# FFN1's pair stage: highs and lows of the tokens in one 512-column matmul, and both halves of a bank added by ScalarE's copy and VectorE

## What is computed

```
x   = x   + 0.5 * m_lat[:, 2] * swiglu(modulate(rms_norm(x,   norm1_g), ...), ffn1_w_in, ffn1_w_out)
ctx = ctx + 0.5 * m_ctx[:, 2] * swiglu(modulate(rms_norm(ctx, norm1_g), ...), ffn1_w_in, ffn1_w_out)

def swiglu(h, w_in, w_out):
    g, u = split(h @ w_in, 2)
    return (silu(g) * u) @ w_out
```

## Time and profile before

| | |
|---|---|
| time, median of 3 runs | 2681.8 us (2681.79 to 2682.47) |
| profiled execution | 2683.84 us, span 2682.0 us |
| TensorE busy | 2632.7 us, 98% of the span |
| VectorE busy | 2134.1 us, 80% |
| ScalarE busy | 1216.8 us, 45% |
| granted TensorE clock, mean | 0.998 |
| the pair stage | 286 to 1016 us of the span |

### The profile page before, as it was taken

The page is one execution under the profiler, slowest core; times in us unless marked ns, Lnnn a source line. Parts: engine busy times, 40 slices in busy tenths (PEclk is TensorE's granted clock), DMA queues, the critical chain, the costliest instruction groups (busy, mean ns, idle before and its releaser), DMA issues.

```text
span 2682.0 us, 37985 instructions
## 1 busy us (share of the span) xinstructions
PE 2632.7 (98%) x15293; PEld 2327.4 (87%) x15293; DVE 2134.1 (80%) x2328; ACT 1216.8 (45%) x1399; POOL 93.7 (3%) x131
## 2 busy tenths in 40 slices
PE   5999999999999999999999999999999999999998
PEld 4778999999999998888888988888988888888887
DVE  6869878788787877899797877586688888888866
ACT  6642344444444443231175543465465455555543
POOL 0000111111111110000000000000000000000000
PEclk9999999999999999999999999999999999999999
DMA  9967699999999888667584585442455555556463
GB/s 309 295 199 211 182 245 249 230 249 250 231 232 258 231 232 289 210 226 243 187 279 135 137 263 189 136 132 79 141 177 194 194 194 197 203 204 206 168 220 125
DMA packets 428939, 558.71 MB, mean 208 GB/s; under 512 B 22274, under 2 KB 280696, under 8 KB 428024
## 3 DMA queue, kind: packets, MB, share of 16 engines
q1 hardware_dynamic: 414156, 504.64, 58.4%
q0 software_dynamic: 14384, 51.92, 10.0%
q10 hardware_dynamic: 252, 0.10, 0.0%
HBM read 505.22 MB, written 13.63 MB: 193 GB/s over the span
## 4 chain that ended last, share of the span: by engine, by line
PE 87%; DVE 4%; ACT 1%; issue 1%; DMA 0%; ACTq 0%; DVEq 0%
PE py L1538 14%; PE py L1540 14%; PE py L1539 14%; PE pg L1538 3%; PE pg L1539 3%; PE pg L1540 3%; PE py L2071 3%; PE py L2073 3%; PE py L2072 3%; PE two L2013 2%; PE two L2015 2%; PE two L2014 2%; PE pu L2052 1%; PE pu L2054 1%; PE pu L2053 1%; PE pu L1538 1%
## 5 line engine op out<-in xcount | busy, mean ns | idle before, releaser
L2455 DVE TENSOR_TENSOR wl<-raw,wh 128x1024 fp32r<-128x1024 f32 x252 | 307.8, 1222 | 111.7 <-ACT wh L1045 111.5
L1045 ACT ACTIVATE wh<-raw 128x1024 fp32r<-128x1024 f32 x252 | 265.7, 1055 | 288.7 <-DVE raw L2459 228.0
L2176 DVE TENSOR_TENSOR wl<-raw,wh 128x2048 fp32r<-128x2048 f32 x101 | 231.1, 2288 | 124.4 <-ACT wh L902 124.2
L1538 PE MATMUL py<-ah,wh 128*128 128x512 f32 (+1 forms) x720 | 277.2, 385 | 0.3 <-issue 0.3
L1539 PE MATMUL py<-al,wh 128*128 128x512 f32 (+1 forms) x720 | 276.8, 384 | 0.0
L1540 PE MATMUL py<-ah,wl 128*128 128x512 f32 (+1 forms) x720 | 276.8, 384 | 0.0
L902 ACT ACTIVATE wh<-raw 128x2048 fp32r<-128x2048 f32 x100 | 190.7, 1912 | 189.0 <-PE py L1540 84.6
L1538 PE MATMUL py<-hh,wh 128*128 128x256 f32 (+1 forms) x752 | 226.1, 301 | 1.8 <-DVE hl L2253 1.0
L1539 PE MATMUL py<-hl,wh 128*128 128x256 f32 (+1 forms) x752 | 224.8, 299 | 0.0
L1540 PE MATMUL py<-hh,wl 128*128 128x256 f32 (+1 forms) x752 | 224.8, 299 | 0.0
L1538 PE MATMUL py<-fhs,wh 128*128 128x256 f32 x720 | 204.0, 283 | 0.4 <-DVE wl L2455 0.4
(11 more groups left out here) (516 smaller groups left out, 7124.9 us busy)
## 6 DMA issues: line engine op xcount, KB each, us to landing
raw<-in_ffn_w_out SPq DMA_DIRECT2D x84, 1024.0 KB, 5.2
chunk<-in_ada_w SPq DMA_DIRECT2D x160, 512.0 KB, 5.5
raw<-in_ffn_w_in SPq DMA_DIRECT2D x144, 512.0 KB, 7.5
raw<-in_ffn_w_in SPq DMA_DIRECT2D x58, 1024.0 KB, 5.1
sraw<-in_ffn_w_in SPq DMA_DIRECT2D x40, 1024.0 KB, 5.1
raw<-raw POOLq DMA_DIRECT2D x72, 512.0 KB, 5.8
raw<-in_ada_w SPq DMA_DIRECT2D x64, 512.0 KB
raw<-in_mix_w_in SPq DMA_DIRECT2D x30, 1024.0 KB
```

The source lines that it names most:

```text
L1045: nc.scalar.activation(wh[:, slot, o:o + 1024], s_half(k, S_SRC[name]), ACT.Copy).then_inc(wh_ready, 1)
L1538: mm(out_ap, w[0], xh_ap, start=first, stop=False, skip_group_check=True)
L2176: tt(wl[:, slot % 2, :], raw[:, slot, :], wh[:, slot % 2, :].bitcast(F32), ALU.subtract).then_inc(wl_ready, 1)
L2455: tt(wl[:, slot, o:o + 1024], s_half(k, S_SRC[forms(k)[pos]]), wh[:, slot, o:o + 1024].bitcast(F32), ALU.subtract).then_inc(wl_ready, 1)
```

## The change

The high and low token tiles become two halves of one tensor (`hhl`, `fhl`), at the same addresses. Of the three matmuls of a tile in the pair stage, the two that have the high weight become one with 512 moving columns: highs of the tokens go to columns 0 to 255 of the bank, lows to columns 256 to 511. The low weight's matmul still adds 256 columns to the first half. The value that was in 256 columns is now the sum of the bank's halves. ScalarE's copies now take the second half, and VectorE adds the first half to it (`both_halves`: `keep_p1`, `keep_p5`, `keep_u2`, `gate_ctx`), and it is this addition that raises `a_p1`, `a_p5`, `a_u2` and `a_x`. `up_ctx`, `up_lat` and `gate_lat` each get a second addition, which waits for the first (`link`). The two silus of a pair become one over 512 columns.

```diff
-    hh = at("hh", [P, 2, KT, LAT], F32R, o_hh)
-    hl = at("hl", [P, 2, KT, LAT], F32R, o_hl)
+    hhl = at("hhl", [P, 2, 2, KT, LAT], F32R, o_hh)
+    hh, hl = hhl[:, 0], hhl[:, 1]
...
-            def pair_keep(k, pos, dst, src, ready):
+            def pair_keep(k, pos, dst, src):
                 se.wait_ge(slab_used, prod(k, pos) + 1)
-                nc.scalar.activation(dst, src[:, 0:LAT], ACT.Copy).then_inc(ready, 1)
-
-            def pair_silu(k):
-                se.wait_ge(slab_used, prod(k, 6) + 1)
+                nc.scalar.activation(dst, src[:, LAT:TOK], ACT.Copy).then_inc(kept, 1)
+
+            def keep_gate(k):
                 if k > FIRST_S:
                     se.wait_ge(act_ready, k)
                 else:
                     se.wait_ge(pu_free, FIRST_S + 1)
-                nc.scalar.activation(sg[:, LAT:TOK], pair_banks(k)[0][:, 0:LAT], ACT.Silu).then_inc(a_x, 1)
+                pair_keep(k, 6, sg[:, LAT:TOK], pair_banks(k)[0])
+
+            def pair_silu(k):
                 se.wait_ge(a_c11, k - FIRST_S + 1)
-                nc.scalar.activation(sg[:, 0:LAT], sg[:, 0:LAT], ACT.Silu).then_inc(a_sg, 1)
+                se.wait_ge(a_x, k - FIRST_S + 1)
+                nc.scalar.activation(sg[:], sg[:], ACT.Silu).then_inc(a_sg, 1)
...
-                    w = (wh[:, slot, o + t * P:o + (t + 1) * P], wl[:, slot, o + t * P:o + (t + 1) * P])
-                    ins = three(bank_[:, 0:LAT], w, xh_ap, xl_ap, first and t == 0, t == HALF - 1)
+                    w_h, w_l = wh[:, slot, o + t * P:o + (t + 1) * P], wl[:, slot, o + t * P:o + (t + 1) * P]
+                    mm(pair(bank_[:]), w_h, both, start=(first and t == 0), stop=False, skip_group_check=True)
+                    ins = mm(bank_[:, 0:LAT], w_l, both[:, 0, :], start=False, stop=(t == HALF - 1), skip_group_check=True)
...
             def up_ctx(k):
                 ve.wait_ge(a_p5, k - FIRST_S + 1)
                 ve.wait_ge(slab_used, prod_of(k, "P7") + 1)
-                tt(tv[:, 1, :], tv[:, 1, :], pair_banks(k)[0][:, 0:LAT], ALU.subtract).then_inc(a_v, 1)
+                x_ = pair_banks(k)[0]
+                link(tt(tv[:, 1, :], tv[:, 1, :], x_[:, 0:LAT], ALU.subtract))
+                tt(tv[:, 1, :], tv[:, 1, :], x_[:, LAT:TOK], ALU.subtract).then_inc(a_v, 1)
...
+            def both_halves(k, n, dst, src, ready):
+                ve.wait_ge(kept, KEPT + 4 * (k - FIRST_S) + n)
+                tt(dst, src[:, 0:LAT], dst, ALU.add).then_inc(ready, 1)
+
+            def keep_p1(k):
+                both_halves(k, 1, p1a[:], pair_banks(k)[0], a_p1)
...
+                    gate_ctx(k - 1)
                     half_low(k, 3)
                     pair_gate(k - 1)
...
                         chunk_step(c_)
                         if ends_round(c_):
                             take_turn(c_, 0)
+                        (keep_p1, keep_p5, keep_u2)[n](k)
                         half_low(k, 4 + n)
```

More of the change, by code:

```diff
@@ L167, in build @@
               for part, n in enumerate(("ah", "al")))
-    fhs, fls = ([at(f"{n}{k}", [P, HALF, LAT], F32R, o + part * 8 * KB) for k, o in enumerate((o_xl, o_xl + 16 * KB, o_a))]
-                for part, n in enumerate(("fhs", "fls")))
+    fhl = [at(f"fhl{k}", [P, 2, HALF, LAT], F32R, o) for k, o in enumerate((o_xl, o_xl + 16 * KB, o_a))]
+    fhs, fls = ([f[:, part] for f in fhl] for part in range(2))
     fht, flt = ([at(f"{n}{k}", [P, HALF, LAT], F32, o + part * 8 * KB) for k, o in enumerate((o_xl, o_xl + 16 * KB, o_a))]
@@ L367, in build @@
     p7_summed, p4_summed = far_loaded, nfb_loaded
+    kept, KEPT = mods_ready, BLOCKS
     lat_done, lat_out, LAT_DONE = xra_ready, xrv_ready, 8
@@ L1069, in _ @@
                 if k > FIRST_S:
+                    keep_gate(k - 1)
+                form_high_half(k, 3)
+                if k > FIRST_S:
                     pair_silu(k - 1)
-                form_high_half(k, 3)
-                pair_keep(k, 0, p1a[:], at_x, a_p1)
+                pair_keep(k, 0, p1a[:], at_x)
                 form_high_half(k, 4)
@@ L1100, in _ @@
             act_high(1)
+            keep_gate(PAIRS - 1)
             pair_silu(PAIRS - 1)
@@ L2471, in up_lat, with keep_p5, keep_u2, gate_ctx @@
                 ve.wait_ge(slab_used, prod(k, 3) + 1)
-                tt(tv[:, 0, :], pair_banks(k)[2][:, 0:LAT], tv[:, 0, :], ALU.subtract).then_inc(a_t12, 1)
+                z_ = pair_banks(k)[2]
+                link(tt(tv[:, 0, :], z_[:, 0:LAT], tv[:, 0, :], ALU.subtract))
+                tt(tv[:, 0, :], z_[:, LAT:TOK], tv[:, 0, :], ALU.add).then_inc(a_t12, 1)
             def gate_lat(k):
                 ve.wait_ge(slab_used, prod_of(k, "P2") + 1)
-                tt(sg[:, 0:LAT], pair_banks(k)[1][:, 0:LAT], p1a[:], ALU.add).then_inc(a_c11, 1)
+                ve.wait_ge(a_p1, k - FIRST_S + 1)
+                y_ = pair_banks(k)[1]
+                link(tt(sg[:, 0:LAT], y_[:, 0:LAT], p1a[:], ALU.add))
+                tt(sg[:, 0:LAT], y_[:, LAT:TOK], sg[:, 0:LAT], ALU.add).then_inc(a_c11, 1)
+            def both_halves(k, n, dst, src, ready):
[3 more added lines that the diff above has]
+                both_halves(k, 1, p1a[:], pair_banks(k)[0], a_p1)
+            def keep_p5(k):
+                both_halves(k, 2, tv[:, 1, :], pair_banks(k)[2], a_p5)
+            def keep_u2(k):
+                both_halves(k, 3, tv[:, 0, :], pair_banks(k)[0], a_u2)
+            def gate_ctx(k):
+                both_halves(k, 4, sg[:, LAT:TOK], pair_banks(k)[0], a_x)
             def pair_gate(k):
@@ L2498, in _ @@
                     last_form(2)
+                    keep_p1(k)
                     half_low(k, 4)
+                    keep_p5(k)
                     half_low(k, 5)
                     form_lo(3)
+                    keep_u2(k)
                     half_low(k, 6)
@@ L2547, in _ @@
             act_low(1)
+            gate_ctx(PAIRS - 1)
             pair_gate(PAIRS - 1)
```

11 lines of the change are left out of this document (5 added, 6 removed).

## The result

The changed kernel takes 2721.9 us (median of four, 2720.4 to 2723.0), the kernel before 2682.0 beside it (2681.8 to 2682.5). The ratio is 1.0148, interval 1.0131 to 1.0166: slower by 1.5%, 10.9 us above the predicted time and inside the range. The profiled execution has 2722.1 us around a span of 2720.2.

A forecast was written before the change was run, and what follows sets the result against it. TensorE bounds the pair stage, but VectorE's longer chain eats the merge's gain. First pair +7.9, 29 plain pairs and 5 with a round's end +19.1, end +2.6: 29.6 us on 2681.8, predicted 2711, range 2694 to 2724.

The forecast's parts named there:

- The mechanism: Pair stage: P6 waits for VectorE's `keep_p1`, `up_ctx` for P7; plain pair 20.24 us against 20.16 before.
- C: Pair stage: chain 0.8 us shorter, plain pairs at TensorE's 19.43 us, rounds' ends stay; 2684 us, no change; chance 0.07.
- D: Pair stage: VectorE's lead covers rounds' ends too, `keep_p1` never late; 34 pairs gain 0.73 us each; 2667 us; chance 0.09.
- Rival A: Pair stage: TensorE's hand-over costs no loop time, VectorE alone sets period 19.83 us; 2699.5 us; chance 0.72 with the forecast.
- Rival B: Pair stage: merged matmul gains nothing, 0.360 us a tile, loop 0.32 us longer; 2720.5 us; chance 0.12.
- The tile: TensorE's products in the pair stage: one 512- and one 256-column matmul take 0.347 us, against 0.360 before.
- The linked additions: VectorE in each pair: two additions, the second waiting for the first, cost 0.80 us.
- Rounds' ends: Pairs in which a round of chunk steps ends: 3.86 us more VectorE work, period 23.69 us, 3.5 more than before.
- The end: Last pair: late `gate_ctx` delays the down projection's second output bank; stage ends 29.6 us later, 2.6 more than at P6.
- K: Start of `keep_p1` in a pair; 9.19 us to `up_ctx`, then 11.05 to the next one in plain pairs.
- It stands still for 0.7 us: Plain pair: TensorE could begin the next P6 at `up_ctx` + 10.83 us, but gets `keep_p1`'s result only at + 11.57.
- 6 to 7 us in the first pair: First pair: TensorE idle before P6, since `keep_p1` stands behind the last form's sum; P6 waits until 298.89 us.

The follow-up runs named there:

- the split kernel: The changed kernel with its 512-column matmul taken apart into two of 256 columns, additions kept: 2722.9 us, ratio to before 1.0152.
- the first pair's keeps: The changed kernel with `keep_p1`, `keep_p5` and `keep_u2` placed earlier in VectorE's order in the first pair: 2715.1 us, ratio 1.0119.
- rounds' ends spread: The changed kernel with a chunk step moved, first and last pairs reordered, and five rounds ending in pairs with one chunk step: 2677.0 us, ratio 0.998.

## Why the prediction was right, and where it was short

**The mechanism held.** P6 waits for `keep_p1` in every pair, by 0.30 to 0.52 us in a plain one (0.7 predicted), and `up_ctx` waits for P7 in nearly all. Only P6 is held in plain pairs. Rivals C and D, in which plain pairs run at TensorE's 19.43, fell. Rival A (TensorE not on the loop) fell by the wait of 0.52 at `up_ctx`, and by the split kernel, whose pair grew by 0.2 when three products in the loop grew. Rival B has nearly the measured number, 2720.5 us, but fell in its cause: the merge alone gains 16 us. So it is in part luck that 2721.9 lies in the range: its upper end of 2724 was there for B and for slower hand-overs, and what filled it was neither.

**The tile was a little too fast.** I took 0.347 us, the lower of two bounds, 0.347 and 0.360. It is 0.353 in most stretches and 0.347 in others; only the mixed sequence itself could show which. That makes the loop longer by 3 x 8 x 0.006 = 0.15 us, hence plain pairs of 20.20 and of 20.36 us, and 2 us more over the stage. By the Trainium skill (TensorE: Matmul & The Clock Gate, Back-to-back issue gap) a merged matmul would save 2.5 ns, by my estimate from its figures. The trace doesn't agree: it saves 7 or 13.

**The linked additions** cost 0.79 us, predicted 0.80. The Trainium skill's statement (VectorE: DVE Perf Modes, The DRAIN you can't avoid) that a semaphore between two VectorE instructions costs nothing extra would have made it 0.68, by my estimate; the starts at 609.00, 609.45 and 609.79 don't agree with it.

**Rounds' ends** took 23.62 (23.69). **The end:** the second output bank came 20.66 us after the last K (20.8).

**The step that failed is a term that the sum lacks: what idle time does to TensorE's clock.** I counted "It stands still for 0.7 us", and "6 to 7 us in the first pair", as that time alone, and every product behind it at the full clock. The stage, up to that second output bank, became 40.1 us longer (284.05 to 1057.34 against 286.21 to 1019.37), where 29.6 were predicted. The difference: K0 to K1 2.8, K1 to K2 2.7, the two pairs behind rounds' ends 2.9, plain pairs some 2. The first three make 8.4 us, and by the windows the stretches at half clock lose 8.2. The Trainium skill (TensorE: Matmul & The Clock Gate, HAM oscillation) says that a kernel whose matmuls come in bursts with gaps between them is set back to the lower clock again and again. The trace agrees in part: there were four stretches in 773 us, each at or behind idle time, but idle pieces as long as some of these (3.08 us in the split kernel, 1.86 in that of the first pair's keeps) had none. The trace of before couldn't show it, since TensorE's longest gap in the stage was 0.97 us.

**Two smaller marks.** VectorE is busy 89% of the stretch from 330 to 1000 us and not 93: waits for ScalarE's high parts remained, 54.8 us from 300 to 1000 us, where the earlier trace rows has 110.4. And nothing came back behind the stage, as said: the medians differ by 39.9 us, the stage by 40.1. (The profiled execution of before lay 2 us above its median and entered the stage 2 us later than that of after.)

## What to carry to other kernels

When work is added to an engine that has room, don't compare its sum with that room: lay out the chain that the bounding engine waits for, and see which of its pieces can move into a hole ahead of it. Here the same additions went with a loss of 40 us or a gain of 10, by the places of a chunk step, some keeps and the rounds' ends. And price a new gap on TensorE with what can follow it: here gaps of 1.8 to 6.8 us went with 3.4 to 10 us at half clock, 8 us beyond the gaps themselves, while the split kernel's gaps of 1.7 to 3.1 us brought none of it.

## What was not expected of the hardware

- **Half clock in a stage in which TensorE is busy 95%.** After idle pieces of 6.8 and 3.4 us, and around rounds' ends with a piece of 1.8 us, stretches of up to 10.4, 7.0, 3.4 and 3.4 us were granted 0.51 or 0.52. Other rounds' ends, and the 0.3 to 0.5 us in each plain pair, left the clock alone. The length of the idle piece before P6 doesn't decide it: 1.83 us went with a stretch twice, while 1.86 and 1.85 at two later rounds' ends (the run with the first pair's keeps earlier), 2.72 in the second pair (rounds' ends spread) and 3.08 (products split) went with none. What does stays open.
- **More work on TensorE cost nothing.** With 2016 matmuls more, the split kernel took the same time, since three of the four stretches at half clock did not come, although its idle pieces there were nearly as long.
- **A tile of one 512- and one 256-column matmul has two speeds**, 0.353 and 0.347 us, both at a granted clock of 1.00. It keeps one over many products. It mostly changes where TensorE had stood still, but with the merge alone it went from 0.353 to 0.347 at 541 us with no two tiles further apart than 0.37 us. The order of the two matmuls doesn't decide it; the cause stays open.
